# Prompt attention with its weights turned four steps behind their scores, and scores taken ahead of the scan chain

## The reference

```python
def dilated_window_attention(q, kc, vc, q_idx, first_valid):
    for window, dil in ((128, 1), (512, 4), (2048, 16)):
        s = q . k / 8, masked to the gathered keys
        ...
    # three branches joined by their softmax denominators

def stick_breaking_attention(q, kc, vc, q_pos, bias):
    z = einsum(q, k) * HEAD_DIM ** -0.5 + bias
    log_beta = where(valid, log_sigmoid(z), -inf)
    log_keep = where(valid, log_sigmoid(-z), 0)
    later = cumsum(log_keep, reverse=True) - log_keep
    a = exp(log_beta + later)
    return einsum(a, v)
```

## Time and profile before

| | us |
|---|---|
| median of 3 runs | 2396.93 (2396.19 to 2397.25) |
| profiled execution, its own time | 2383.74 |
| its span, first to last instruction | 2382.1 |
| TensorE busy | 2262.2 (95%) |
| weight loads of TensorE busy | 2056.9 (86%) |
| VectorE busy | 1198.0 (50%) |
| ScalarE busy | 925.7 (39%) |
| GpSimd busy | 146.3 (6%) |
| mean granted TensorE clock | 0.978 |
| HBM | 274.99 MB read, 13.58 MB written |

### The profile page before, as it was taken

One profiled execution on the slowest core, in us unless ns is written; L12 is line 12 of the kernel. 1 busy time (PEld: TensorE's weight loads), 2 busy tenths in 40 slices (PEclk: granted clock), 3 DMA queues, 4 the chain that ended last, 5 costly groups with the idle time before them and its releaser, 6 DMA issues. The chain is left out here.

```text
span 2382.1 us, 44896 instructions
## 1 busy us (share of the span) xinstructions
PE 2262.2 (95%) x17646; PEld 2056.9 (86%) x17646; DVE 1198.0 (50%) x2114; ACT 925.7 (39%) x1637; POOL 146.3 (6%) x197
## 2 busy tenths in 40 slices
PE   7999999999898899999999999999998898999997
PEld 7999999777656699999999999987775667999997
DVE  6434265426666565432454333762467664743425
ACT  6223342324426654323352233432244474622333
POOL 0000010002222000000000000100113300000000
PEclk8999999999989999999999999999999998999999
DMA  5223334216867632232323333441468755422333
GB/s 141 78 70 88 103 104 136 87 64 188 265 184 212 208 107 72 80 96 77 102 73 95 82 88 89 123 131 53 125 197 255 243 150 184 104 74 70 91 104 93
DMA packets 384958, 290.97 MB, mean 122 GB/s; under 512 B 51808, under 2 KB 368393, under 8 KB 384273
## 3 DMA queue, kind: packets, MB, share of 16 engines
q1 hardware_dynamic: 368128, 234.08, 34.7%
q0 software_dynamic: 16128, 54.54, 7.3%
q10 hardware_dynamic: 528, 0.02, 0.0%
HBM read 274.99 MB, written 13.58 MB: 121 GB/s over the span
## 5 line engine op out<-in xcount | busy, mean ns | idle before, releaser
L222 PE MATMUL ps<-h_hi,w_hi 128*128 128x288 f32 x2400 | 716.8, 299 | 16.0 <-PEq L177 10.3
L223 PE MATMUL ps<-h_lo,w_hi 128*128 128x288 f32 x2400 | 708.5, 295 | 0.0
L224 PE MATMUL ps<-h_hi,w_lo 128*128 128x288 f32 x2400 | 708.2, 295 | 0.0
L222 PEld LDWEIGHTS ps<-h_hi,w_hi 128*128 128x128 f32 x2400 | 450.5, 188 | 23.3 <-issue 16.6
L246 DVE TENSOR_TENSOR w_lo<-w_raw,w_hi 128x2048 fp32r<-128x2048 f32 x143 | 327.7, 2292 | 260.9 <-ACT w_hi L240 260.5
L223 PEld LDWEIGHTS ps<-h_lo,w_hi 128*128 128x128 f32 x2400 | 450.7, 188 | 1.0
L224 PEld LDWEIGHTS ps<-h_hi,w_lo 128*128 128x128 f32 x2400 | 450.6, 188 | 0.0
L240 ACT ACTIVATE w_hi<-w_raw 128x2048 fp32r<-128x2048 f32 x143 | 272.9, 1908 | 129.0 <-PE ps L224 77.5
L222 PE MATMUL ps<-f_a_hi,w_hi 128*128 128x288 f32 x1024 | 302.7, 296 | 0.0
L224 PE MATMUL ps<-f_a_hi,w_lo 128*128 128x288 f32 x1024 | 301.6, 295 | 0.0
L223 PE MATMUL ps<-f_a_lo,w_hi 128*128 128x288 f32 x1024 | 301.5, 294 | 0.0
(11 more groups left out here) (365 smaller groups left out, 3203.4 us busy)
## 6 DMA issues: line engine op xcount, KB each, us to landing
w_raw<-in_w_ffn_in SPq DMA_DIRECT2D x132, 512.0 KB, 5.2
w_raw<-in_w_ffn_out SPq DMA_DIRECT2D x80, 512.0 KB, 4.5
sa_vn<-in_cache_sb_v SPq DMA_DIRECT2D x256, 128.0 KB
w_raw<-in_w_in SPq DMA_DIRECT2D x52, 512.0 KB, 4.4
sa_vn<-in_cache_win_v SPq DMA_DIRECT2D x96, 128.0 KB
w_raw<-in_w_out SPq DMA_DIRECT2D x24, 512.0 KB, 8.1
sa_kn_early<-in_cache_win_k POOLq DMA_DIRECT2D x72, 128.0 KB
sa_vn<-in_cache_win_v SPq DMA_DIRECT2D x16, 512.0 KB
```

Of the source, the lines that this page charges most:

```text
L222: pe.matmul(out, stat_hi, mov_hi, start=start, stop=False, skip_group_check=True)
L223: pe.matmul(out, stat_hi, mov_lo, start=False, stop=False, skip_group_check=True)
L224: return pe.matmul(out, stat_lo, mov_hi, start=False, stop=stop, skip_group_check=True)
```

## The change

The number of draining steps goes from 5 to 6, so there are 38 steps, and the plan of the side ticks is computed anew from the longer list (`ORDER` takes its last stretch from the length of `PROMPT_STEPS`). Weights are turned at step u + 4 instead of u + 3; the product, the tile's rows and ScalarE's copy of turned weights follow from `prompt_plan` and move by one step as well. On VectorE the take of score t is issued ahead of the scan chain of unit t - 2 instead of behind it. On ScalarE the order within a step stays as it was. `SPLIT_STEP` stays the third-last step. Nothing else is changed: no instruction is added or removed.

```diff
@@ -2124,7 +2124,7 @@
-PROMPT_STEPS = [i + 1 for i in range(PT_TILES) for _ in range(2 * H)] + [2] * 5
+PROMPT_STEPS = [i + 1 for i in range(PT_TILES) for _ in range(2 * H)] + [2] * 6
 SPLIT_STEP = len(PROMPT_STEPS) - 3
@@ -2133,7 +2133,7 @@
     for u, (i, h, kind) in enumerate(PROMPT_UNITS):
-        t = u + 3
+        t = u + 4
         turn_at.setdefault(t, []).append(u)
         out_at.setdefault(t + 1, []).append(u)
@@ -2298,17 +2298,6 @@
         for t in range(G["ticks"]):
-            u = t - 2
-            if 0 <= u < len(units) and units[u][2] == "stick":
-                s, w = nth[u], width(u)
-                zu, fu = z[:, u % PZ, 0:w], f[:, s % PF, 0:w]
-                dve.wait_ge(S["ln_done"], s + 1)
-                dve.scalar_tensor_tensor(fu, zu, 0.0, fu, ALU.max, ALU.add).then_inc(S["f_done"], 1)
-                dve.wait_ge(S["f_done"], s + 1)
-                dve.tensor_tensor_scan(fu[:, ::-1], one[:, 0:1].to_broadcast([P, w]), fu[:, ::-1], 0.0,
-                                       ALU.mult, ALU.add).then_inc(S["sum_done"], 1)
-                dve.wait_ge(S["sum_done"], s + 1)
-                dve.tensor_tensor(zu, zu, fu, ALU.subtract).then_inc(S["scanned"], 1)
             if t < len(units):
                 i, h, kind = units[t]
@@ -2325,6 +2314,17 @@
                     dve.scalar_tensor_tensor(zt[:, w - P:w], score_bank(t)[:, w - P:w], bias[:, h:h + 1], strict[:],
                                              ALU.add, ALU.add).then_inc(S["z_ready"], 1)
+            u = t - 2
+            if 0 <= u < len(units) and units[u][2] == "stick":
+                s, w = nth[u], width(u)
+                zu, fu = z[:, u % PZ, 0:w], f[:, s % PF, 0:w]
+                dve.wait_ge(S["ln_done"], s + 1)
+                dve.scalar_tensor_tensor(fu, zu, 0.0, fu, ALU.max, ALU.add).then_inc(S["f_done"], 1)
+                dve.wait_ge(S["f_done"], s + 1)
+                dve.tensor_tensor_scan(fu[:, ::-1], one[:, 0:1].to_broadcast([P, w]), fu[:, ::-1], 0.0,
+                                       ALU.mult, ALU.add).then_inc(S["sum_done"], 1)
+                dve.wait_ge(S["sum_done"], s + 1)
+                dve.tensor_tensor(zu, zu, fu, ALU.subtract).then_inc(S["scanned"], 1)
```

## The result

The changed kernel took 2424.09 us (median of 4 runs, 2422.82 to 2429.16) against 2396.56 us of the kernel before beside it (4 runs, 2395.98 to 2397.25): ratio 1.0129, 95% interval 1.0105 to 1.0152. It is 27.5 us slower, outside the forecast range, on the side to which the forecast leaned. Every time and ratio here leaves out two slow runs, one of e3 (7615 us) and one of e4 (6775 us).

A forecast was written before the change was run, and what follows sets the result against it. TensorE, busy 2262.2 of 2382.1 us, was taken as the bound, so only its waits could be won. Seven terms summed to +2.0 us per layer, +4.1 in two, moving the 2396.93 us median to 2401; range 2389 to 2409.

The forecast's parts named there:

- Term 1: Prompt attention: most of TensorE's wait for VectorE's stick-score take goes, as ticks move to odd steps; -2.1 us per layer.
- Term 2: Steps 15/16, 19/20, 21/22, 25/26: ScalarE's late key copy makes TensorE wait for keys; +3.7 us per layer.
- Term 3: Transposes of steps 13 and 19 wait for ScalarE's late copy of turned weights; +1.15 us per layer.
- Term 4: Step 13's sample take behind the chain, 0.35, and value unit 42's late sample-weight copy, 0.85; +1.2 us per layer.
- Terms 5 to 7: Score ahead of value unit 31's page, -0.5; late work filling V-load holes, -0.9; last exponential's wait gone, -0.5 us.
- term 7: End of attention: the last unit's chain precedes its turn by two steps, so line 2363's wait goes; -0.5 us.
- B: Rival: the take wait moves to line 2320 at about 2.9 us, ScalarE's copies stay hidden; 2393 us, chance 0.20.
- C: Rival: no take is late and ScalarE has the slack; -4.4 us per layer, 2388 us, chance 0.20.
- D: Rival: new holes halve TensorE's clock once per layer in steps 25 to 28; +5.4 us per layer, 2408, chance 0.14.

The follow-up runs named there:

- e3: Kernel before with only the take moved ahead of the scan chain on VectorE (37 steps, three-step turn, old tick plan): 2398.47 us, ratio 1.0078.
- e4: Kernel before with weights turned four steps behind, an added step of weight 0, old tick plan, chain ahead of the take: 2385.65 us, ratio 1.0009.
- e8: Changed kernel, shifted tick plan kept, with ScalarE's last stick exponential one step later (unit t - 3): 2391.25 us, ratio 1.0024 to the kernel before.
- e2: Kernel before with one empty draining step of weight 2 added, so only the side ticks shift: 2387.73 us, ratio 1.0019.
- e5_after_again: Changed kernel, unedited, measured again on another chip: 2410.45 us, ratio 1.0105 to the kernel before.
- e1: Changed kernel with weight 0 for the added step, so side ticks sit as before: 2402.35 us, ratio 1.0079 to the kernel before.
- e7: Changed kernel with the old tick plan and ScalarE's last stick exponential one step later (unit t - 3): 2390.12 us, ratio 1.0025 to the kernel before.

## Why the prediction was wrong

**What held.** The mechanism: the wait for the take goes, and the chain, now 2 us later, makes ScalarE and through it TensorE late; e8 confirms the second half. Of the signs named in advance, no wait is left on the stick take's last instruction; 1.1 us stand on the window take (called: under 1); ScalarE idles ahead of line 2363 for 22 us per layer (over 10); TensorE's waits on line 2755 are 5.6 us (3 to 5), the longest 1.7 (1.4); step 24's score starts 69.5 us after score 0 against 66.7 (no earlier).

**Term 1** (-2.1): measured -2.8, from 3.9 to 1.1 us. Right, slightly too careful. The ticks' new places decide it, as the forecast says: they alone bring the wait to 0.9 us in each layer (e2). The new order alone does so too (e3, 0.9), both together with no more.

**Term 2** (+3.7): the four pairs of steps waited 0.93, 0.86, 0.98 and 1.06 us (forecast 1.4, 0.9, 0.75 and 1.3), together 3.8, less the 0.6 of before: +3.2. The timings by which it was worked out stand in the timeline above: key copy 5.73 us after the score (forecast 5.8), keys at 6.45 (6.5), wait 0.86 (0.95).

**Term 3** (+1.15): 0.69 us in step 7, which was not named, 0.17 in step 19 (forecast 0.5) and none in step 13 (0.65); but 2.5 us at one transpose of the tail, which the forecast did not follow, since it worked the steps only as far as the pairs with keys. **Term 4** (+1.2): the sample take cost nothing more (1.3 us before and after). The late copy of sample weights (line 2763) at step 28 was right as a cause, but its first reader is not the value unit (0.85 forecast): it is the gather, line 2723, with 1.9 us.

**The first step that failed** is thus the list of who waits behind ScalarE. "A copy that had over a microsecond in hand makes TensorE wait about 0.95" was applied to the next keys and to turned weights; the gather was left out. It waited 1.7 us for the key copy and 1.9 for line 2763; with the product's 0.6 for line 2367 and the tail's 2.5 this makes 5.9 us per layer with the 0.85 of term 4 taken off. Terms 5 to 7 (-1.9 together) brought 0 at the page of value unit 31 (2.2 to 2.1 us) and -2.0 at the window pages (2.8 in the earlier trace rows, to 0.8); term 7's 0.5 went, and the tail's 2.5 came. Term by term that is -2.8 + 3.2 + 0.9 + 1.9 + 1.7 + 0.6 + 2.5 - 2.6 = +5.4 us in the first layer, and idle time of attention and tail rose by 5.5 (15.3 to 20.8), where the forecast had +2.0. That terms 5 to 7 come out near their size is luck in part: with the fourth step alone (e4) the page waits are 4.6 and 5.4 us in attention and tail of the two layers, against 4.9 and 4.1 before. So the fourth step does not shorten them; that a TensorE late for other reasons finds the pages there is the likely reason, not tested.

**The second step that failed** is "A tick placed one entry later in the earlier mixers (...) costs nothing while pages are there; bounds -1 to +1 us per layer, taken as 0". Pages were not what decided. In the kernel before, keys of a tick fill the hole in which TensorE waits for ScalarE's copy ahead of line 1825; one entry later they come behind it. At this place the wait is 0.8 us in both layers before and 2.7 in both layers of `e5_after_again`. Kernel before:

```profile
564.88 1.04 PE L2642 MATMUL ps<-ident,sa_kn_early 128*128 128x128 f32 x8
...
567.75 0.33 PE L1825 MATMUL ps<-ml_left,ident 64*64 64x64 f32 x2 [0.83 <-ACT ml_left L1770]
```

and the changed kernel:

```profile
569.42 0.33 PE L1825 MATMUL ps<-ml_left,ident 64*64 64x64 f32 x2 [2.74 <-ACT ml_left L1770]
...
570.32 1.04 PE L2642 MATMUL ps<-ident,sa_kn_early 128*128 128x128 f32 x8
```

Idle time ahead of attention is 15.8 to 18.9 us in all twenty layers profiled with the early ticks in their old places (ten kernels), and 19.6 to 24.1 in all eight with the shifted plan (e2, e8 and two profiles of the changed kernel). At a like clock (0.96) it is 17.6 against 21.7: +4 per layer. In time it is less: that stretch lasts 174.4 to 183.5 us in the twenty, on average 179.3, and 181.1 to 182.9, on average 181.8, in e2, `e5_after_again` and e8 (191.2 and 187.6 in the first comparison). These 2.5 us per layer, still outside the bounds, agree with e2, which has nothing else: +0.19%, or 4.5 us in two layers.

**The rivals.** B (the wait changes its name only) and C (it does what it says) fell: the name changed and 2.8 us went, and the ScalarE copies were not hidden. D put the loss into new half-clock stretches. They came: the clock in attention fell from 1.00 to 0.97 and busy time rose 3.4 us, the size that D gave one stretch. But they are not what carries the loss. e3 loses 0.78% and kept clock 1.00 and 0.98 in attention, the kernel before's own values; e2 and e8 have 0.95 to 0.98 there and ratios of 1.0019 and 1.0024. The first layer of e3, then of e2 (columns as in the earlier trace rows):

```profile
698.57:801.36 102.79, 86.50 (x932) 61.32 (x931) 60.12 (x154) 60.59 (x158) 17.04 (x30) 1.00 0.62 185
```
```profile
705.03:801.10 96.07, 87.35 (x932) 64.11 (x931) 63.07 (x157) 61.99 (x158) 17.04 (x30) 0.96 0.70 198
```

The Trainium skill, TensorE: Matmul & The Clock Gate, What's actually happening, has an idle array fall to half rate. Whether small holes bring that about these rows do not tell: e3 idled 16.3 us there at clock 1.00, e2 8.7 us at 0.96. Over the whole kernel the mean clock was nearly the same with and without the change (0.9763 and 0.9767). What stays open is the rest of the 7.3 us by which TensorE's busy time rose in the pair of profiles. In e1 (0.9750 against 0.9780 over its runs) the clock may be some 4.5 us of 18, at the 1.5 us per 0.001 given below; that was not isolated.

**The sum, as measured.** By stage, `e5_after_again` less before, both layers: ahead of attention -1.3 and +5.0, attention +7.9 and +7.3, tail +3.1 and +3.5, together 25.5 of the 26.2 us by which the spans differ. Idle time is 19.9 us of it, busy time 5.6. In the first layer ahead of attention the clock hides the loss: before had 0.91 there against 0.95, so busy time fell by 6.7 us while idle time rose by 5.4. By cause: order through ScalarE's queue 0.55% with the plan of before (e1 to e7) and 0.8% with the shifted one (e5 to e8), plan 0.2%. The 0.15 to 0.25% for order through VectorE's queue was seen with the plan of before only; in the changed kernel the wait for the sample take did not grow (1.3 us before and after), so its share there is not shown. The two comparisons of the whole change gave 1.05% and 1.29%; why the first is larger stays open (its runs have clocks of 0.971 and 0.972, and those of the kernel before beside it are not on record), as does the depth's part within 0.1%.

## What to carry to other kernels

Moving an instruction up in one queue moves another down; follow the one moved down to its reader on the next engine, and list everything that is queued behind that reader, with all its own readers, not only the next one of the same kind. Here the right companion of the swap was to move ScalarE's exponential one step later too, which took back three quarters of the loss with one digit. And a plan that spreads work in proportion to a sum moves all of it when one weight is added at the end: compare its placements before and after, and look for those that filled a hole. Last, try each part of a change alone: the shifted ticks took the wait that the swap was meant to take, at 0.2% instead of 1%.

## What was not expected of the hardware

The same program differs between executions by its mean granted clock. In 29 runs of the kernel before on one chip it lay between 0.972, with a span of 2393.9 us, and 0.981, with 2378.2: a line through all of them falls by 1.5 us per 0.001. A single profile can therefore lie several us off its median. Whether the 13 us of the profile ahead of the prediction came this way is not shown: the clocks of the three runs beside it are not on record, and its 2383.74 us lies within 2 us of the medians of the kernel before on the four other chips (2384.38 to 2385.71). Two layers of one execution, with the same instructions, show it too: 183.0 us ahead of attention at clock 0.91, 176.5 at 0.96; and the idle time moves the other way (15.8 and 17.6 us). The same holds for the twenty layers with the early ticks in their old places: 15.8 us in the eight at clock 0.91, 17.5 to 18.9 in the other twelve, at 0.93 to 0.97. That at half clock TensorE is busy for longer and its releasers are therefore less late is my reading, not tested. Idle times are only to be compared at a like clock.
